# First stage reordered with x read two groups ahead; gate and memory work spread beside the forgetting heads up to the last 60 units

## The chip, the cores and the metric

The kernel runs on all 8 cores of one Trainium2 chip. Each core computes one of the 8 batch entries, with its own copy of the weights, and the cores exchange nothing. The metric is the device time in microseconds (us) of the slowest core. On a core five engines work in their own order: TensorE (PE in the profile, its weight loads PEld), VectorE (DVE), ScalarE (ACT), GpSimd (POOL), and SyncE (SP), which here only issues DMAs. An engine's queue is served in program order: an instruction that waits holds everything behind it on its engine, DMA issues included.

## What is computed

A decoder layer over 4096 tokens of width 1024: three parallel token mixers, a gated merge, an output projection and a squared-ReLU MLP.

```python
h = rmsnorm(x, g_mix[l])
proj = h @ w_in[l]                                            # (B, T, IN_WIDTH)
qa, ka, va, qb, kb, vb, fl, qm = jnp.split(proj, offs, axis=-1)
# mixer A: three groups of dilated sliding windows, merged by softmax denominators -> ya
# mixer B: forgetting attention, 8 heads, causal over all 4096 tokens
logf = jax.nn.log_sigmoid(fl.astype(jnp.float32) + b_f[l].astype(jnp.float32))
yb = fox_attention(qb, kb, vb, logf).astype(dt)
# memory cross-attention: 4 heads over 256 memory tokens -> ym
gates = jax.nn.sigmoid(h @ w_gate[l] + b_gate[l]).reshape(B, T, N_BRANCH, D)
merged = (gates[:, :, 0] * (ya @ w_br_a[l])
          + gates[:, :, 1] * (yb @ w_br_b[l])
          + gates[:, :, 2] * (ym @ w_br_m[l]))
x = x + merged @ w_out[l]
h2 = rmsnorm(x, g_mlp[l])
x = x + jnp.square(jax.nn.relu(h2 @ w_up[l])) @ w_down[l]
```

In `fox_attention` the logits of query t and key s get the sum of the log forget gates between them; the kernel adds it through six extra rows of the query and key operands, which is why its score matmuls have 70 rows.

## The kernel before

Every instruction is recorded by helpers (`MM`, `ACT`, `TT`, `STT`, `COPY`, `P.dma`; lines 238 to 268, DMAs line 59), so the profile shows their lines. `Prog.finalize` derives the semaphore waits from reads and writes. On each engine the order is the order in which the program text emits the instructions. On-chip memory is one arena of 205 KB per partition, cut by hand with `at(kb, columns)`: a new tile waits for all users of the tiles that lay there. `wcast` is a DMA issued by POOL that reads f32 weights from memory and writes bf16.

The stages on the core whose trace is shown:

- **First stage**, `phase_a` (0 to 310 us): eight token groups (`tg`) of 512 tokens. For a group, `load_x` brings eight f32 tiles of x (2 MB), `squares` squares them on ACT and sums them on POOL (chunks 0 to 4) and DVE (5 to 7) with two scratch tiles `sqs` used in turn, and ends with a sum and two roundings `shi`, `slo` on DVE; `norm` sums over partitions with two matmuls and forms 1/rms (ACT Ln, Exp); `scale` writes the bf16 `hT` with eight DVE instructions. `vproj(i, js)` multiplies a 128-token tile of `hT` by the value weights in three column blocks of 512, 256 and 512 (8 matmuls each, five banks in turn), copies them to a staging tile `vst`, and stores that to `vsc`. `p2_tg` computes the cumulated log forget gates of a group: 8 matmuls, ACT Exp and Ln, a scan and six more small instructions on DVE, and two stores to `augsc` issued by POOL. `ones_out` issues six constant stores from POOL, once. At group 4 the rotary tables (4 MB, SP) and two column groups of weights (POOL) are loaded as well.
- **Query and key projections, dilated attention** (310 to 857 us), which the change doesn't touch. The memory tokens are loaded and prepared at its start (`mem_prep`).
- **The joint loop** (857 to 1646 us): `run(...)` takes steps from several generators so that all advance in proportion: seven forgetting heads (`fox_heads(0, 7)`, 7 x 144 units), the gates (`gates`, 768 steps), memory attention (`mem_attn`, 140) and the casts of the MLP weights (`wprep`, 16). A unit of a head is a score matmul, an exponential on ACT and a value matmul. A head goes through 8 query groups of 512 tokens; group tg has 4 tg + 4 units, the last four of them narrower (512, 384, 256, 128 columns) and masked on POOL. At the end of a query group DVE takes a reciprocal and a product. Scores run three units ahead of the value matmuls.
- **The last head and the first group's merge** (1646 to 1792 us): `wcast` of the three branch weights and of `w_out`; 16 units of head 7 alone; loads of gates (`load_g`) and of the branch inputs (`load_y`); 28 more units alone; then the last 100 units beside `head_d`, that is `br_stage(0)` (eight output chunks of 2, 4 and 4 matmuls, each product with a gate on DVE, two sums on POOL) and `out_stage(0)` (eight chunks of 8 matmuls, residual sum, squares, norm, scale).
- **Rest** (1792 us to the end): the MLP with the merges of the following groups.

## Time and profile before

| | us |
|---|---|
| timed runs, in order | 3376.24, 3373.81, 2918.67 |
| their median | 3373.81 |
| the profiled execution | 2917.94 |
| its span, slowest core (the one shown below) | 2916.4 |
| spans of the 8 cores | 2897.2 to 2916.4 |
| mean granted TensorE clock, by core | 0.972 to 0.976 |

| stage | from, to (us) | PE busy |
|---|---|---|
| groups 0 to 6 of the first stage | 38.88 to 284.82 | 166.88 of 245.94 |
| projections, dilated attention | 310.04 to 856.84 | 498.99 of 546.80 |
| joint loop | 856.84 to 1645.88 | 777.85 of 789.04 |
| last head and first merge | 1645.88 to 1791.69 | 105.74 of 145.81 |
| rest, after the first 27 us | 1818.65 to 2916.40 | 1090.06 of 1097.75 |

Times count from the first instruction. The granted clock is 1.00 where TensorE runs at the upper of its two levels, 2.4 GHz, and 0.50 at 1.2 GHz. The value in brackets behind an instruction is the time its engine was idle before it, with what ended that. Matmuls overlap in the trace, so a busy share near 1 can still hide a lower clock.

### The profile page before, as it was taken

The page shows a single profiled execution, that of the slowest core. Times are in us where ns is not written, and L with a number is a line of the kernel's source. Part 1 is how long each engine was busy: PE and PEld are TensorE (multiplying, and loading weights), DVE is VectorE, ACT ScalarE, POOL GpSimd, SP SyncE. Part 2 cuts the span into 40 slices and gives each one's busy share as a digit, 9 for nine tenths or more (in the row PEclk, how much of TensorE's full clock was granted, in tenths as well). Part 3 has the DMA queues.
Part 4 walks back from the last instruction along what each step waited for, and adds up shares of the span by engine and source line. Part 5 has one row for each costly group of instructions (what it writes and reads, how often), then busy time and mean ns, then how long its engine had stood idle before and what let it go on. Part 6 is the DMA issues. An engine that isn't in the chain of part 4 may idle for free.

```text
span 2916.4 us, 45239 instructions; the slowest of 8 cores (2897.2 to 2916.4 us)
## 1 busy us (share of the span) xinstructions
PE 2687.6 (92%) x12800; PEld 1204.4 (41%) x12800; DVE 1329.3 (46%) x1761; ACT 1435.3 (49%) x2649; POOL 672.2 (23%) x770
## 2 busy tenths in 40 slices
PE   3667999998979999999999877999999999999999
PEld 1323444343434444444444322444444444444444
DVE  3444566677764655555646533323333333323221
ACT  2333455799988888887888743212121212111120
POOL 2211343343331111111101132222222222222200
PEclk9878999999999999999999989999999999999999
DMA  5363433563564454354333553464646464646353
GB/s 120 126 178 120 108 73 74 151 163 113 141 117 100 92 103 99 76 106 93 82 74 80 104 156 131 138 208 142 214 145 206 154 211 140 216 148 210 111 177 101
DMA packets 204929, 386.56 MB, mean 133 GB/s; under 512 B 82688, under 2 KB 143104, under 8 KB 181760
## 3 DMA queue, kind: packets, MB, share of 16 engines
q1 hardware_dynamic: 150640, 320.95, 34.8%
q0 software_dynamic: 51600, 56.39, 11.9%
q10 hardware_dynamic: 2448, 6.33, 0.8%
q8 instruction: 112, 1.84, 0.3%
q14 instruction: 129, 1.06, 0.1%
HBM read 328.31 MB, written 110.89 MB: 151 GB/s over the span
## 4 chain that ended last, share of the span: by engine, by line
PE 85%; DMA 4%; ACT 3%; DVE 3%; issue 2%; POOL 2%; SPq 1%; ACTq 0%; DVEq 0%; POOLq 0%
PE bank L238 85%; ACT arena L244 3%; POOL arena L247 2%; DMA arena<-xT 1%; DMA arena<-wsc_up 1%; DVE arena L257 1%; SPq L59 1%; DVE arena L261 1%; DMA arena<-ysc 1%; DVE arena L247 1%; DMA arena<-w_in 1%; DMA out<-arena 0%; DMA arena<-mem 0%; ACTq L59 0%; DMA qksc<-arena 0%
## 5 line engine op out<-in xcount | busy, mean ns | idle before, releaser
L238 PE MATMUL bank<-arena 128*128 128x512 bf16 (+6 forms) x12444 | 2629.5, 370 | 119.8 <-DVE arena L257 43.4
L238 PEld LDWEIGHTS bank<-arena 128*128 128x128 bf16 (+3 forms) x12444 | 1173.6, 98 | 1538.9 <-issue 299.7
L244 ACT ACTIVATE arena<-bank 128x512 bf16<-128x512 f32 (+2 forms) x1926 | 1012.2, 570 | 878.9 <-PE bank L238 865.8
L247 DVE TENSOR_TENSOR arena<-bank,arena 128x512 f32<-128x512 f32 (+2 forms) x528 | 373.1, 712 | 536.0 <-PE bank L238 498.7
L247 POOL TENSOR_TENSOR arena<-arena 128x512 f32<-128x512 f32 (+1 forms) x264 | 358.4, 1358 | 971.6 <-DVE arena L247 483.8
L247 DVE TENSOR_TENSOR arena<-arena 128x512 bf16<-128x512 bf16 (+5 forms) x392 | 213.7, 545 | 501.6 <-ACT arena L244 470.9
L247 POOL TENSOR_TENSOR arena<-arena,cb_sb 128x128 bf16<-128x128 bf16 (+2 forms) x352 | 212.9, 616 | 869.0 <-ACT arena L244 864.1
L244 ACT ACTIVATE arena<-arena 128x512 f32<-128x512 f32 (+2 forms) x352 | 217.2, 626 | 331.0 <-DVE arena L247 270.4
L261 DVE RECIPROCAL arena<-bank 64x512 f32<-64x512 f32 (+1 forms) x96 | 322.1, 3355 | 63.7 <-PE bank L238 61.7
L244 ACT ACTIVATE arena<-bank,gcols 128x512 f32<-128x512 f32 (+1 forms) x364 | 249.6, 686 | 202.7 <-PE bank L238 187.7
L238 PE MATMUL bank<-arena,cb_sb 128*128 128x512 bf16 (+1 forms) x340 | 110.8, 391 | 103.8 <-DVE arena L264 88.0
L253 DVE TENSOR_SCALAR arena<-arena 128x512 bf16<-128x512 f32 x192 | 82.1, 430 | 270.1 <-ACT arena L244 268.9
L257 DVE SCALAR_TENSOR_TENSOR arena<-bank,gcols,arena 128x512 bf16<-128x512 f32 (+1 forms) x196 | 152.7, 800 | 100.7 <-ACT arena L244 56.2
L257 DVE SCALAR_TENSOR_TENSOR arena<-arena,gcols 128x512 bf16<-128x512 f32 x128 | 91.0, 748 | 28.3 <-ACT arena L244 23.1
L238 PEld LDWEIGHTS bank<-arena,cb_sb 128*128 128x128 bf16 x340 | 33.3, 98 | 166.9 <-issue 135.8
L59 POOL DMA_DIRECT2D out<-arena x64 | 35.3, 552 | 289.2 <-DVE arena L247 287.1
L247 DVE TENSOR_TENSOR arena<-arena,cb_sb 128x512 bf16<-128x512 bf16 (+1 forms) x96 | 49.0, 510 | 10.0 <-ACT arena L244 6.2
L264 DVE CAST arena<-bank 128x256 bf16<-128x256 f32 x32 | 13.4, 420 | 46.8 <-PE bank L238 46.6
L59 POOL DMA_DIRECT2D augsc<-arena x22 | 12.4, 569 | 81.7 <-DVE arena L264 58.0
L264 DVE COPY arena<-bank 128x512 f32<-128x512 f32 x32 | 30.4, 1027 | 0.0
L59 POOL DMA_DIRECT2D arena<-w_gate x24 | 21.7, 909 | 24.6 <-PE bank L238 24.6
L264 DVE CAST arena<-arena 8x512 bf16<-8x512 f32 (+1 forms) x40 | 16.8, 420 | 10.9 <-POOL arena L247 7.1
(24 smaller groups left out, 61.4 us busy)
## 6 DMA issues: line engine op xcount, KB each, us to landing
arena<-wsc_up SPq DMA_DIRECT2D x64, 1024.0 KB, 5.8
arena<-wsc_dn SPq DMA_DIRECT2D x64, 1024.0 KB, 6.0
arena<-xT SPq DMA_DIRECT2D x128, 256.0 KB, 7.5
gsc<-arena SPq DMA_DIRECT2D x192, 128.0 KB, 2.0
arena<-gsc SPq DMA_DIRECT2D x64, 384.0 KB, 6.5
arena<-qksc SPq DMA_DIRECT2D x16, 1024.0 KB, 8.6
out<-arena POOLq DMA_DIRECT2D x64, 256.0 KB, 5.0
vsc<-arena SPq DMA_DIRECT2D x32, 480.0 KB, 2.7
```

The source lines that it names most:

```text
L59: self.op(eng, lambda e: e.dma_start(out=out, in_=in_, **kw), reads, writes, dma=True, nobar=nobar)
L238: P.op("pe", lambda e: e.matmul(out, lhsT=lhsT, rhs=rhs, start=start, stop=stop), reads, writes)
L244: P.op("act", lambda e: e.activation(out=out, in_=in_, func=func, **kw), reads, writes)
L247: P.op(eng, lambda e: e.tensor_tensor(out=out, in0=in0, in1=in1, op=op), reads, writes)
L253: P.op(eng, lambda e: e.tensor_scalar(out=out, in0=in0, scalar1=s1, scalar2=s2, op0=op0, op1=op1), reads, writes)
L257: P.op("dve", lambda e: e.scalar_tensor_tensor(out=out, in0=in0, scalar=scalar, in1=in1, op0=op0, op1=op1), reads, writes)
L261: P.op("dve", lambda e: e.reciprocal(out=out, in_=in_), reads, writes)
L264: P.op(eng, lambda e: e.tensor_copy(out=out, in_=in_), reads, writes)
```

## The change

In the first stage, x is read one group earlier (`load_x(tg + 2)` at the top of group tg, into the same two buffers). The squares of the next group come ahead of each of the first two `vproj`, `norm` comes after the first block of the third tile, `scale` in one piece after the third tile, and `p2_tg` at the end of the group. All three copies of a tile go to ACT, and there are three staging tiles. The constant row is shorter and read four times by a broadcast DMA.

In the joint loop all 8 heads take part, up to all but the last 60 units; the casts of two of the three branch weights are inside the loop (`wbr_early`). Behind it, `load_y(0)`, the cast of the first branch weight and three `load_g` come at once, then 16 units alone, `load_x(0)` and the cast of `w_out`, and the last 44 units beside `head_d`. The gate tiles and two product tiles move to the place of `hT`.

```diff
@@ phase_a
-        onesr, r_onesr = at1(181, T)
-        vst, r_vst = zip(*[at(189 + 4 * i, 1920, n=4) for i in range(2)])
+        onesr, r_onesr = at1(183, 1024)
+        vst, r_vst = zip(*[at(185 + 4 * i, 1920, n=4) for i in range(3)])
@@ ones_out
-                P.dma(augsc[:, 0, 3 + j, :], onesr[0:8, :], reads=[r_onesr], writes=[ra_[-1]], eng="pool")
+                o4 = onesr[0:8, :].unsqueeze(1).to_broadcast([8, 4, 1024])
+                P.dma(augsc[:, 0, 3 + j, :].rearrange("h (a t) -> h a t", a=4), o4, reads=[r_onesr], writes=[ra_[-1]],
+                      eng="pool")
@@ vproj
-                if j == 1:
-                    COPY("dve", dst, src, [rb[bk]], [r_vst[i % 2][j]])
-                else:
-                    ACT(dst, src, AF.Copy, [rb[bk]], [r_vst[i % 2][j]])
-            P.dma(vsc[i * 128:(i + 1) * 128], v, reads=list(r_vst[i % 2]), writes=[r_vsc[i]])
+                ACT(dst, src, AF.Copy, [rb[bk]], [r_vst[i % 3][j]])
+            if 2 in js:
+                P.dma(vsc[i * 128:(i + 1) * 128], v, reads=list(r_vst[i % 3]), writes=[r_vsc[i]])
@@ group loop
-            if tg:
-                load_x(tg + 1)
+            load_x(tg + 2)
             if tg == 2:
                 ones_out()
             if tg == 4:
                 load_group(0)
                 load_group(1)
                 load_tabs()
+            squares(tg + 1, 0)
             vproj(4 * tg, (0, 1, 2))
-            squares(tg + 1, 0)
+            squares(tg + 1, 1)
             vproj(4 * tg + 1, (0, 1, 2))
-            squares(tg + 1, 1)
+            vproj(4 * tg + 2, (0,))
+            norm(tg + 1)
+            vproj(4 * tg + 2, (1, 2))
+            scale(tg + 1, 0, 8)
+            vproj(4 * tg + 3, (0, 1, 2))
             p2_tg(tg)
-            norm(tg + 1)
-            vproj(4 * tg + 2, (0, 1, 2))
-            scale(tg + 1, 0, 4)
-            vproj(4 * tg + 3, (0, 1, 2))
-            scale(tg + 1, 4, 8)
@@ joint loop and what follows
-    fx = fox_heads(0, 7)
-    run((rest(fx), 7 * 144), (gt, 768), (mem_attn(), 140), (wprep(), 16))
+    wbr = [None, at(120, 4 * 1024), at(128, 4 * 1024)]
+    def wbr_early():
+        yield 1
+        for b, w_d in ((1, w_brb_d), (2, w_brm_d)):
+            wcast(wbr[b][0].rearrange("p (k c) -> p k c", k=4), w_d.rearrange("(k p) c -> p k c", p=128), [wbr[b][1][0]])
+            yield 1
+    ALONE, LAST = 16, 44
+    fx = fox_heads(0, 8)
+    nf = 8 * 144 - ALONE - LAST
+    run((take(fx, nf), nf), (gt, 768), (mem_attn(), 140), (wprep(), 16), (wbr_early(), 5))
-    Gt = [at1(120 + 3 * i, 1536) for i in range(4)]
+    Gt = [at1(4 + 3 * i, 1536) for i in range(4)]
-    wcast(wbr[:, 0:2], w_bra_d.rearrange("(k p) c -> p k c", p=128), [r_wbr[0]])
-    wcast(wbr[:, 2:6], w_brb_d.rearrange("(k p) c -> p k c", p=128), [r_wbr[1]])
-    wcast(wbr[:, 6:10], w_brm_d.rearrange("(k p) c -> p k c", p=128), [r_wbr[2]])
-    wcast(wo, w_out_d.rearrange("(k p) c -> p k c", p=128), [r_wo])
-    last = fox_heads(7, 8)
-    for _ in range(16):
-        next(last)
+    load_y(0)
+    wcast(wbr[0], w_bra_d.rearrange("(k p) c -> p k c", p=128), [r_wbr[0]])
     for n in range(3):
         load_g(n)
-    load_y(0)
-    for _ in range(28):
-        next(last)
+    for _ in take(fx, ALONE):
+        pass
     load_x(0)
+    wcast(wo, w_out_d.rearrange("(k p) c -> p k c", p=128), [r_wo])
-    tt_ = [at1(132 + 2 * i, 512, F32) for i in range(3)]
+    tt_ = [at1(kb, 512, F32) for kb in (16, 18, 136)]
-    run((rest(last), 100), (head_d(), 44))
+    run((rest(fx), LAST), (head_d(), 44))
```

## Rows read from the trace of the kernel before

**Rows 1.** The page, busy us of each engine over the whole span.

```profile
PE 2687.6 (92%) x12800; PEld 1204.4 (41%) x12800; DVE 1329.3 (46%) x1761; ACT 1435.3 (49%) x2649; POOL 672.2 (23%) x770
```

**Rows 2.** First stage by token group: window, length, busy of each engine, clock, DMA share, GB/s.

```profile
38.88:76.59 37.71, 26.33 (x106) 11.55 (x107) 16.19 (x24) 11.49 (x20) 6.26 (x6) 0.86 0.41 119
76.59:108.14 31.55, 23.11 (x107) 10.95 (x108) 16.16 (x24) 11.46 (x20) 9.26 (x12) 0.84 0.42 134
...
176.34:220.41 44.07, 23.47 (x107) 10.85 (x107) 15.52 (x24) 11.69 (x20) 6.25 (x6) 0.77 0.74 215
...
253.41:284.82 31.41, 22.22 (x106) 10.54 (x107) 16.22 (x24) 11.61 (x20) 6.19 (x6) 0.89 0.38 129
284.82:310.04 25.22, 25.22 (x124) 12.53 (x125) 6.03 (x11) 7.28 (x12) 2.05 (x3) 0.93 0.28 100
```

**Rows 3.** First stage, timeline of PE: start, length, instruction, count, idle before it.

```profile
94.89 0.59 PE L238 MATMUL bank<-arena,cb_sb 128*128 128x512 bf16 x1 [5.98 <-DVE arena L264]
...
96.06 9.83 PE L238 MATMUL bank<-arena 128*128 128x512 bf16 x48
...
239.88 11.28 PE L238 MATMUL bank<-arena 128*128 128x512 bf16 x48
```

**Rows 4.** The chain of work in time order, group 1: first and last link shown.

```profile
87.73 0.63 ACT arena L244
...
93.52 0.70 DVE arena L247
```

**Rows 5.** First stage, timeline: the norm's two ACT instructions, and eight scale instructions.

```profile
96.36 0.69 ACT L244 ACTIVATE arena<-bank,gcols 128x512 f32<-128x512 f32 x1 [4.05 <-PE bank L238]
...
97.14 0.63 ACT L244 ACTIVATE arena<-arena 128x512 f32<-128x512 f32 x1
```
```profile
31.98 6.75 DVE L257 SCALAR_TENSOR_TENSOR arena<-arena,gcols 128x512 bf16<-128x512 f32 x8 [2.35 <-ACT arena L244]
```

**Rows 6.** First stage, timeline: scan of the forget gates, and POOL's stores behind it.

```profile
63.11 1.21 DVE L450 TENSOR_TENSOR_SCAN arena<-arena 8x512 f32<-8x512 f32 x1
...
68.77 1.22 POOL L59 DMA_DIRECT2D augsc<-arena  x2 [7.77 <-DVE arena L251]
...
101.23 4.22 POOL L59 DMA_DIRECT2D augsc<-arena  x8 [7.88 <-DVE arena L264]
```

**Rows 7.** First stage: SP's issue of the first two groups of x; their landing.

```profile
1.50 43.62 SPq L59 DMA_DIRECT2D arena<-xT  x16
```
```profile
arena<-xT SPq DMA_DIRECT2D x128, 256.0 KB, 7.5
```

**Rows 8.** Joint loop and last head: windows, columns as in rows 2.

```profile
856.84:1645.88 789.04, 777.85 (x3713) 355.24 (x3713) 424.26 (x363) 654.80 (x1252) 116.54 (x253) 1.00 0.43 91
1645.88:1683.64 37.76, 22.66 (x92) 7.89 (x92) 20.73 (x11) 22.36 (x49) 9.59 (x20) 0.80 0.98 171
1683.64:1742.00 58.36, 49.56 (x195) 19.47 (x196) 24.41 (x28) 28.34 (x54) 23.37 (x24) 0.87 0.55 168
1742.00:1791.69 49.69, 33.52 (x147) 13.05 (x146) 15.74 (x16) 27.02 (x53) 11.95 (x15) 0.96 0.03 8
```

**Rows 9.** PE lines by form, 2000 to 2900 us: count, busy us, mean ns.

```profile
L238 PE MATMUL bank<-arena 128*128 128x512 bf16 x4160 | 899.0, 379 | 0.0
```

**Rows 10.** Behind the joint loop, timeline of PE: units of head 7 alone.

```profile
1649.67 10.96 PE L238 MATMUL bank<-arena 128*128 128x512 bf16 x40 [2.62 <-POOL arena L247]
```

**Rows 11.** DMA issues from 1663.7 to 1669 us: count, size, us to landing.

```profile
arena<-ysc SPq DMA_DIRECT2D x2, 512.0 KB, 24.6
```

**Rows 12.** First merge, timeline of POOL: first sum of two successive chunks.

```profile
1722.03 1.27 POOL L247 TENSOR_TENSOR arena<-arena 128x512 f32<-128x512 f32 x1
...
1726.30 1.26 POOL L247 TENSOR_TENSOR arena<-arena 128x512 f32<-128x512 f32 x1 [0.77 <-DVE arena L247]
```

**Rows 13.** End of the first output stage: its last residual sum; MLP's first matmuls.

```profile
1779.37 0.69 DVE L247 TENSOR_TENSOR arena<-bank,arena 128x512 f32<-128x512 f32 x1 [4.39 <-PE bank L238]
```
```profile
1791.69 22.14 PE L238 MATMUL bank<-arena 128*128 128x512 bf16 x84 [4.78 <-DVE arena L257]
```

More of the change, by code:

```diff
@@ L433, in ones_out @@
                 ra_.append(R())
-                P.dma(augsc[:, 0, 3 + j, :], onesr[0:8, :], reads=[r_onesr], writes=[ra_[-1]], eng="pool")
+                o4 = onesr[0:8, :].unsqueeze(1).to_broadcast([8, 4, 1024])
+                P.dma(augsc[:, 0, 3 + j, :].rearrange("h (a t) -> h a t", a=4), o4, reads=[r_onesr], writes=[ra_[-1]],
+                      eng="pool")
                 ra_.append(R())
-                P.dma(augsc[:, 1, j, :], onesr[0:8, :], reads=[r_onesr], writes=[ra_[-1]], eng="pool")
+                P.dma(augsc[:, 1, j, :].rearrange("h (a t) -> h a t", a=4), o4, reads=[r_onesr], writes=[ra_[-1]],
+                      eng="pool")
         def p2_tg(tg):
@@ L505, in vproj @@
         def vproj(i, js):
-            v = vst[i % 2]
+            v = vst[i % 3]
             for j in js:
@@ L527, in phase_a @@
         MEMSET("pool", onesr[0:8, :], 1.0, [r_onesr])
-        for i in range(2):
+        for i in range(3):
             MEMSET("pool", vst[i][:, :, 64:128], 1.0, [r_vst[i][3]])
@@ L1131, in rest @@
             yield c
-    fx = fox_heads(0, 7)
-    run((rest(fx), 7 * 144), (gt, 768), (mem_attn(), 140), (wprep(), 16))
-    wbr, r_wbr = at(0, 10 * 1024, n=3)
-    wbr = wbr.rearrange("p (k c) -> p k c", k=10)
+    wbr = [None, at(120, 4 * 1024), at(128, 4 * 1024)]
[8 more added lines that the diff above has]
+    run((take(fx, nf), nf), (gt, 768), (mem_attn(), 140), (wprep(), 16), (wbr_early(), 5))
+    wbr[0] = at(0, 2 * 1024)
+    r_wbr = [w[1][0] for w in wbr]
+    wbr = [w[0].rearrange("p (k c) -> p k c", c=1024) for w in wbr]
+    Gt = [at1(4 + 3 * i, 1536) for i in range(4)]
     wo, r_wo = at1(20, 8 * 1024)
@@ L1208, in br_stage @@
                 for kc in range(k0, k1):
-                    MM(banks[bk][:, :], wbr[:, kc, c * 128:(c + 1) * 128], yti[:, kc, :], kc == k0, kc == k1 - 1,
+                    MM(banks[bk][:, :], wbr[br][:, kc - k0, c * 128:(c + 1) * 128], yti[:, kc, :], kc == k0, kc == k1 - 1,
                        [r_wbr[br], r_yti[br]], [rb[bk]])
```

## The prediction

> **What bounds the kernel now.** I read the page first: PE is busy 92% of the span, the next engine 49% [rows 1]. So the kernel is bound by matmuls wherever its order lets it be, and the question is where PE waits. The windows by stage answer that. The joint loop keeps PE busy 777.9 of 789.0 us at a granted clock of 1.00 [rows 8]; nothing is to be had there. Two stretches are loose. In the first stage a group takes 31.4 to 44.1 us, with PE busy 22 to 26 at a clock of 0.77 to 0.89 [rows 2]. Behind the loop, 1645.88 to 1791.69 us, PE is busy 105.7 of 145.8 at 0.80 to 0.96 [rows 8]. The change works on just these two.
>
> The unit of cost is a full matmul of 512 columns: 899.0 us for 4160, 0.216 us each at the upper clock level, 2.4 GHz [rows 9]; narrower ones I count by their columns.
>
> A first-stage group holds 4 tiles of 20 full matmuls, 8 for the forget gates and 2 for the norm, 90 x 0.216 = 19.4 us. The shortest normal group takes 31.4 [rows 2]. The rest is a gap of 6 us before the norm's matmuls [rows 3] (seven of these, 6 to 18 us, the long ones behind a late x), one of 2.2 us before each new group, for the second half of `scale`, and the lower clock behind the gaps: the 48 matmuls that follow a norm are 40 full ones, 8.6 us, and take 9.8 to 11.3 [rows 3] (mean of the seven 10.4), 1.8 us too long.
>
> **First stage after the change.** Let 0 be the end of the gate matmuls of the group before; they now come last in their group. I follow the chain that leads to the next norm, queue by queue.
>
> - ACT: Exp and Ln of the forget gates, like the norm's pair 1.4 us with their hop [rows 5]; the scan starts at 1.55.
> - POOL: the stores of `p2_tg` now stand ahead of the squares' sums of the next group in POOL's queue, where before they came behind both halves. From the scan's start to the end of the two issues it is 68.77 + 1.22 - 63.11 = 6.9 us [rows 6]. POOL is held until 8.45, though ACT's first squares are done at 4.
> - The first sum ends at 9.8. The square of chunk 2 needs its scratch tile, so ACT resumes then; the copies of tile 1 wait behind it, which the five banks cover.
> - From that square to the norm's first matmul the old chain takes 94.89 - 87.73 = 7.2 us [rows 3, 4]. Nothing in it changes: first norm matmul at 17.0, both done 1.4 later at 18.4.
> - PE has had 48 x 0.216 = 10.4 us of work by then (two tiles and a block), so it still waits some 6 us here. The gap has not gone.
> - Behind it 40 full matmuls, 8.6 us, and the 1.8 us of the clock: 28.8.
> - DVE: Ln starts 1.5 us after the first norm matmul, Exp ends at 2.9 [rows 3, 5], then 0.1 + 6.75 + 0.15 for eight scale instructions [rows 5]: 26.8. That is hidden under the matmuls: the 2.2 us gap is gone, and 26.8 is the lower bound of the period.
>
> So a period of 28.8 us (26.8 to 31.5, the old normal one) for 31.4. The greater gain is that x no longer comes late: it has a whole group to land, and lands in 7.5 us [rows 7].
>
> Group 0: the second x is issued until 45.1 [rows 7] and its needed chunks land near 50 (an estimate). ACT now squares it ahead of all copies: 2.2, three copies 1.6, so chunk 2 at 53.8; with 7.2, 1.4 and 8.6 + 1.8, group 1 starts at 72.8 (for 76.59; 69 if x doesn't hold ACT). Six periods, 172.8. In group 2 six constant stores, 4.22/8 x 6 = 3.2 us [rows 6], and in group 4 two casts, taken as 1.8, stand in POOL's queue ahead of the sums too; both lay hidden before. The four times shorter pieces of the broadcast store I cost at nothing; POOL's issue is what counts. In group 4 the tables (4 MB) still stand ahead of the stores of the value tiles; in 44.1 us the old group moved 9.5 MB [rows 2], so the first store lands near 27, and the third staging tile lets ACT go on until about 24: 3 us (0 to 8). Group 7 starts at 72.8 + 172.8 + 8.0 = 253.6 for 284.8: **31.2 us gained**.
>
> Copies moved to ACT: its busy time grows from 11.5 by 4 x 0.4 us, half of the period; nothing. Forget gates last: in group 7 they delay the next stage, since the memory tokens are loaded over their tiles; at most the 5.7 us of that chain [rows 6], I take **4 lost**. The DVE part of it is over before the first projection needs DVE.
>
> **Behind the loop.** A head has 132 full units (144 units counted by columns). The 84 units that move into the loop are 75 of these, 150 matmuls: 32.4 us; the loop is 98.6% busy, so it grows by 33. ACT adds 84 x 0.55 = 46 to 654.8 of 789.0 us: 85% of 822, still no bound. The two early casts cost POOL an issue each.
>
> The remainder, from the end of the gates to the first MLP matmul:
>
> - 16 units alone, 20 take 10.96 [rows 10]: 8.8. The wait of 2.6 us before them (masks behind four casts on POOL) goes, since these units have no mask.
> - Wait for the branch inputs: landing took 24.6 us [rows 11] with three gate loads ahead and the casts beside it, 2.4 MB in all. Now they go first, 1.25 MB: 12.8 us. Issued at 3, landed at 16, gates of the first chunk at 17: a wait of 8 (0 to 15).
> - `br_stage`: a chunk with its three units is 16 matmuls, 3.5 us. But the product tile of a chunk is freed by two POOL sums one after the other: sum 1.27, 0.2, sum 1.27, then two DVE products of 0.7 and hops, 4.3 us; two successive chunks are 1726.30 - 1722.03 = 4.3 apart [rows 12], the least seen. Eight at 4.5, with one reciprocal and four masks of 4 in all: 40 (36 to 53; 53 is the mean pace of before, 6.6 a chunk).
> - `out_stage`: 8 x 12 matmuls, 20.7, say 22; two units a chunk instead of 4.5, so the wait for the exponentials, 1 us a chunk, should go (if not, 30).
> - End: 1791.69 - 1779.37 = 12.3 us [rows 13], of which 6.9 were units; now some 4.2: 9.7.
>
> Sum 33 + 8.8 + 8 + 40 + 22 + 9.7 = 121.5 for 145.8: **24.3 us gained** (3 to 40). Then up to 1818 the MLP waits for its third weight tile, loaded behind the same queue: no change.
>
> On the shared transfer the Trainium skill ("DMA: Bandwidth & Descriptors", Queues, rings and completion order) says that each DMA engine goes round between the queues that have work, packet by packet. By that rule the branch inputs get half of what moves, and at the 171 GB/s of that window [rows 8] 1.25 MB take 14.6 us (an estimate) for the 12.8 of the row: the sum would be 1.8 us longer.
>
> **Total.** 31.2 - 4 + 24.3 = 51.5; 2917.9 - 51.5 = **2866 us**. The profiled execution, 2917.9, stands 456 us below the median shown, 3373.8, and 0.7 below the shortest of the three runs; the forecast is for executions like it.
>
> **Rivals.**
>
> 1. POOL doesn't hold the squares (its sums come earlier than I count). Then the chain's start moves from 9.8 to about 5.5, the period is 24.5, and group 4 and 2 lose nothing: 6 x 4.3 + 5 = 31 more, **2835**. For: PE needs only 19.4. Against: the order in POOL's queue is plain.
> 2. The tail gives back nothing: branch inputs and `w_out` come later, and a chunk keeps its 6.6 us with fewer units beside it. 15 + 53 + 30 instead of 8 + 40 + 22: 28 less, **2894**. For: PE and DMA waits of before at the same place, DMA share 0.98 [rows 8].
> 3. The first stage keeps its normal 31.5 us a group and gains only the late x: 6 x 2.7 = 16 less, **2882**.
> 4. Slower: the denser loop and MLP, 822 + 1098 us, no longer get the upper clock throughout. It turns the sign when 1920 x (1/c - 1) passes 51.5, at a mean clock of 0.974; at the 0.93 that the densest first-stage window shows [rows 2] it costs 145, **3011**. Against: 789 us at 98.6% busy ran at 1.00 [rows 8].
>
> **How the numbers follow.** My forecast 0.51, rivals 0.14, 0.16, 0.14 and 0.05. The range leaves out rival 4 and the outer edges: 2833 to 2896. A measurement can tell 2% from no change, 58 us, so "faster" begins at 2860: rival 1 with 0.13 and the lower part of my own case (2848 to 2884), 0.24, give 0.37. Rivals 2 and 3 and the rest, 0.58. Slower, 0.05.
>
> **What will show it.** In the trace after: starts of groups some 29 us apart; before the norm's matmuls a gap of about 6 us still, and POOL's first sum right behind its two stores, 8 us into the group; no gap at the group's start; PE's clock there still below 0.9. Group 7 near 254 us. The loop ends 33 us later relative to its start; first MLP matmul 122 - 33 = 89 us after the gates' end; chunk sums on POOL 4.3 to 5 us apart. I am wrong if POOL sums before its stores, if the gap before the norm is under 3 us, or if the branch inputs land after 20 us.

## The result

The changed kernel takes 2911.19 us (median of 20 runs, 2896.75 to 3258.92), the kernel before 2931.51 beside it; ratio 0.9939 with a 95% interval of 0.9917 to 0.9962. A gain of 18 us for a forecast of 52: the same within 2%, and outside my range of 2833 to 2896. Some executions are longer, at a lower granted clock on the cores of one die or both (the 3258.92 is one); the ratios leave them out, and of e13, whose profile is one, only the cores of the other die are read. The profiled execution took 2914.3 us, its slowest core 2912.8; on the others the span is 2878.1 to 2906.6.

The page of the kernel after, busy time by engine, for [rows 1]:

```profile
PE 2686.5 (92%) x12548; PEld 1211.2 (42%) x12800; DVE 1313.5 (45%) x1729; ACT 1443.7 (50%) x2681; POOL 672.3 (23%) x771
```

This row can't tell the two kernels apart, so the stages must. I cut each trace at four marks that all kernels here have: the first norm matmul of the projections, the first matmul of head 0 behind PE's 5.2 us wait for ACT, the issue of the `w_br_a` cast on POOL (it waits for the last gate matmul), and the first MLP matmul. Each number is the mean over the eight cores of the profiled execution, in us.

| kernel | first stage | projections, windows | loop | behind it | MLP | span |
|---|---|---|---|---|---|---|
| before | 307.3 | 534.4 | 802.4 | 145.3 | 1116.8 | 2906.1 |
| after | 280.8 | 544.6 | 850.5 | 101.1 | 1121.1 | 2898.1 |
| after, profiled again (e8) | 277.8 | 539.0 | 851.5 | 100.8 | 1120.7 | 2889.8 |
| e8 less before | -29.5 | +4.6 | +49.1 | -44.5 | +3.9 | -16.3 |
| forecast | -31.2 | +4 | +33 | -57.3 | 0 | -51.5 |

(The forecast's two loop terms: the loop grows by 33, the stage behind it shrinks from 145.8 to 88.5.) The 35 us between forecast and e8 are mainly two terms: 16 in the loop, 13 behind it; the MLP has 4. Each row is one execution, and that of before is a short one: its mean span is 2906.1, where the executions of before in the ratios of the runs below have 2911.1 to 2915.8. So differences to the row of before come out 5 to 10 us too small in sum; in which stage isn't known.

The first profile of after has 544.6 us in its second column, 6 more than e8 of the same kernel. The windows of 300 to 560 us, on core 2 and on core 5 (columns as in [rows 2]):

```profile
300.00:560.00 260.00, 247.08 (x1104) 106.74 (x1125) 162.41 (x226) 144.51 (x259) 100.06 (x65) 0.92 0.43 97
300.00:560.00 260.00, 244.85 (x1195) 105.55 (x1193) 167.08 (x236) 155.48 (x280) 103.87 (x71) 0.98 0.42 96
```

Core 2 shows 0.92 of the clock and fewer instructions in the same time, core 5 shows 0.98. In e8, the same kernel, all cores show 0.98 or 0.99, so the change doesn't bring it about every time; e17 and e18 below have it on some cores again. What sets it is open. Behind the first stage I read after from core 5.

**First stage.** Timeline of PE, after, core 2 (columns as in [rows 3]):

```profile
61.88 0.38 PE L238 MATMUL bank<-arena,cb_sb 128*128 128x512 bf16 x1 [4.13 <-DVE arena L264]
...
90.58 0.59 PE L238 MATMUL bank<-arena,cb_sb 128*128 128x512 bf16 x1 [6.63 <-DVE arena L264]
...
91.83 21.82 PE L238 MATMUL bank<-arena 128*128 128x256 bf16 x102
123.56 0.59 PE L238 MATMUL bank<-arena,cb_sb 128*128 128x512 bf16 x1 [9.91 <-DVE arena L264]
```

and POOL and ACT ahead of the norm at 90.58:

```profile
80.73 1.22 POOL L59 DMA_DIRECT2D augsc<-arena  x2 [20.46 <-DVE arena L247]
81.95 1.30 POOL L247 TENSOR_TENSOR arena<-arena 128x512 f32<-128x512 f32 x1
```
```profile
83.34 1.15 ACT L244 ACTIVATE arena<-arena 128x512 f32<-128x512 f32 x2 [4.75 <-POOL arena L247]
```

The norms of groups 1 to 7 stand at 61.88, 90.58, 123.56, 152.19, 184.01, 213.25 and 243.16: periods of 28.7, 33.0, 28.6, 31.8, 29.2 and 29.9 us, 181.3 in all. POOL's sum starts the moment its two stores are issued, ACT waits 4.75 us for it, and PE 6.63 before the norm. Behind the norm PE runs without a break: the 2.2 us gap at a group's start is gone. Group 7 starts at 255.1 us here and at 252.2 on core 5 of e8 (forecast 254).

**Loop.** Windows from the loop's first to its last matmul, after, core 5:

```profile
815.95:1668.53 852.58, 826.75 (x3915) 375.89 (x3916) 454.01 (x379) 701.12 (x1350) 134.69 (x288) 0.99 0.42 90
```

In before PE was idle for 12.6 us in this stretch of core 5 (786.87 of 799.47 busy), now for 25.8. What PE waited for there: engine, releaser, us in total, times, longest. Before:

```profile
PE bank L238 <- ACT arena L244: 10.7, 9, 5.2
PE bank L238 <- POOL arena L247: 6.0, 12, 2.2
PE bank L238 <- DVE arena L261: 0.4, 2, 0.2
```

After:

```profile
PE bank L238 <- ACT arena L244: 11.2, 9, 5.2
PE bank L238 <- DVE arena L247: 10.0, 8, 3.7
PE bank L238 <- POOL arena L247: 7.6, 15, 2.9
PE bank L238 <- DVE arena L261: 1.8, 2, 0.9
```

What is new is DVE: 11.8 us for 0.4. The timeline of DVE and of PE at one such wait, core 5:

```profile
1265.48 3.35 DVE L261 RECIPROCAL arena<-bank 64x512 f32<-64x512 f32 x1
...
1269.73 3.36 DVE L261 RECIPROCAL arena<-bank 128x512 f32<-128x512 f32 x1
...
1273.58 3.36 DVE L261 RECIPROCAL arena<-bank 64x512 f32<-64x512 f32 x1
```
```profile
1277.94 6.34 PE L238 MATMUL bank<-arena 128*128 128x512 bf16 x21 [2.06 <-DVE arena L247]
```

The 64-row ones are the head's own, at the end of its token groups; the 128-row one belongs to the memory attention and has come between two of them. PE waits for the product behind the third.

**Behind the loop.** Timeline of PE, after, core 5; the gates end at 1668.53:

```profile
1669.43 7.52 PE L238 MATMUL bank<-arena 70*128 70x512 bf16 x30 [0.32 <-ACT arena L244]
1687.07 1.86 PE L238 MATMUL bank<-arena 128*128 128x512 bf16 x4 [10.12 <-DMA arena<-ysc]
1693.20 2.72 PE L238 MATMUL bank<-arena 128*128 128x512 bf16 x6 [4.26 <-DMA arena<-ysc]
1698.33 6.77 PE L238 MATMUL bank<-arena 128*128 128x512 bf16 x22 [2.42 <-DVE arena L247]
...
1738.47 20.42 PE L238 MATMUL bank<-arena 128*128 128x512 bf16 x95 [0.58 <-DVE arena L247]
...
1768.39 6.82 PE L238 MATMUL bank<-arena 128*128 128x512 bf16 x12 [4.67 <-DVE arena L257]
```

The units alone take 8.4 us (forecast 8.8). From their end at 1676.95 to 1698.33, where the branch stage begins to flow, are 21.4 us (forecast a wait of 8). The branch stage, counted from there, takes 40.1 (forecast 40), the output stage 20.4 (22), its end 9.5 (9.7). The issue of the branch inputs on SP and their landing, for [rows 11]:

```profile
1673.91 0.45 SPq L59 DMA_DIRECT2D ysc<-arena  x1
1674.51 1.78 SPq L59 DMA_DIRECT2D arena<-ysc  x3
```
```profile
arena<-ysc SPq DMA_DIRECT2D x2, 512.0 KB, 20.4
```

They are issued 6.0 us behind the gates' end, right behind a store in SP's queue, on all eight cores (forecast 3), and the last of the three lands 18.0 to 22.2 us later, by core (forecast 13). The two DMA queues from issue to landing, 1674.5 to 1694.9 us: packets, MB, share of the engines' time; software is POOL's queue with its casts, hardware is SP's.

```profile
q0 software_dynamic: 1051, 2.11, 70.2%
q1 hardware_dynamic: 1675, 1.93, 34.7%
```

### The profile page after: what moved, and what is told of

Its sections match the earlier page's. It is cut to its first block, busy times and chain, and to the rows that moved or that the text cites. A ratio compares the mean times of both kernels' runs of the same rounds, so it can differ in the third digit from the quotient of the medians.

```text
span 2912.8 us, 45013 instructions; the slowest of 8 cores (2878.1 to 2912.8 us)
## 1 busy us (share of the span) xinstructions
PE 2686.5 (92%) x12548; PEld 1211.2 (42%) x12800; DVE 1313.5 (45%) x1729; ACT 1443.7 (50%) x2681; POOL 672.3 (23%) x771
## 4 chain that ended last, share of the span: by engine, by line
PE 83%; DVE 4%; DMA 4%; ACT 3%; issue 3%; POOL 2%; SPq 0%; ACTq 0%; DVEq 0%; POOLq 0%
PE bank L238 83%; ACT arena L244 3%; POOL arena L247 2%; DVE arena L261 2%; DVE arena L247 1%; DMA arena<-xT 1%; DMA ysc<-arena 1%; DMA arena<-gsc 1%; DMA arena<-wsc_up 1%; DVE arena L264 0%; SPq L59 0%; DVE arena L257 0%; POOL augsc L59 0%; DVE arena L453 0%; DMA qksc<-arena 0%
## 5 line engine op out<-in xcount | busy, mean ns | idle before, releaser
L238 PEld LDWEIGHTS bank<-arena 128*128 128x128 bf16 (+2 forms) x12444 | 1179.3, 99 | 1530.0 <-issue 330.6
L244 ACT ACTIVATE arena<-bank 128x512 bf16<-128x512 f32 (+3 forms) x1958 | 1021.4, 567 | 830.3 <-PE bank L238 808.5
L244 ACT ACTIVATE arena<-arena 128x512 f32<-128x512 f32 (+3 forms) x352 | 216.3, 626 | 353.5 <-DVE arena L247 260.5
L244 ACT ACTIVATE arena<-bank,gcols 128x512 f32<-128x512 f32 (+2 forms) x364 | 249.8, 686 | 212.2 <-PE bank L238 193.7
L453 DVE TENSOR_TENSOR_SCAN arena<-arena 8x512 f32<-8x512 f32 x8 | 10.1, 1264 | 45.6 <-ACT arena L244 45.6
```

Of the source, the lines that this page charges most:

```text
L238: P.op("pe", lambda e: e.matmul(out, lhsT=lhsT, rhs=rhs, start=start, stop=stop), reads, writes)
L244: P.op("act", lambda e: e.activation(out=out, in_=in_, func=func, **kw), reads, writes)
L453: P.op("dve", lambda e: e.tensor_tensor_scan(out=cs_, data0=sp_, data1=sp_, initial=init, op0=ALU.add, op1=ALU.max), rd, [r_csb[k]])
```

## Which half of the change gains: e1, e2, e8

The kernel before with the new first stage only (e1), and with the new loop and stage behind it only (e2). e8 is the changed kernel again.

> The kernel before with the first stage of the change alone. Theory (my steps for the first stage held, the loss is behind it): the joint loop starts 30 us earlier, as in the changed kernel (826 against 857 us on an undisturbed core), and nothing behind it moves, so the time falls by 27 to 31 us, ratio 0.990. Rival (part of the stage's gain is given back later, by what is now nearer behind it): the loop starts 30 us earlier but the end comes only about 20 us earlier, ratio 0.993.

> The kernel before with the joint loop and what follows of the change, first stage as before. Theory (the 84 units moved cost the loop more than their matmuls, and the branch inputs land late): the loop takes 842 us for 789, the stretch behind it 100 for 146, so the time is 7 us longer, ratio 1.0025, between 1.000 and 1.005. Rival (these losses come from the new first stage, which shifts the cores against each other): loop 822, stretch 89 to 100, the time 14 to 24 us shorter, ratio 0.992 to 0.995.

> The changed kernel once more, beside the others on the same chip. Theory: 20 to 26 us shorter than the kernel before, ratio 0.991 to 0.993, the same as its undisturbed cores showed (2890 against 2916 us). Rival (its 0.9939 holds a cost of its own that undisturbed cores don't show): 0.994 or more again.

e1: ratio 0.9897 (0.987 to 0.9924), 2895.5 us, first stage 277.8 for 307.3, next column 538.2 for 534.4. e2: ratio 1.0022 (0.9999 to 1.0045), loop 850.3 for 802.4, behind it 101.5 for 145.3, MLP 1121.4 for 1116.8. e8 has two executions that can be compared, 2905.67 (the profiled one) and 2899.36 us, beside 2923.68 for before: 18 and 24 us less, and no ratio of its own. So the first stage gains what was forecast (-29.5 + 3.8 for -31.2 + 4), and the rest of the change, worth 24.3 us in the forecast, gives nothing: 47.9 - 43.8 + 4.6, some 9 us lost by the stages, 0 to 13 by the ratio's interval. In e1 the loop, which it doesn't change, takes 805.1 for 802.4.

## The loop: e5, e6, e7, e14

e5 and e6 take the memory attention's 32 reciprocals out of the kernel after and of the kernel before (its output is then not normalised):

```diff
-            RECIP(rec, banks[dk][:, :], [rb[dk]], [r_rec])
+            COPY("dve", rec, banks[dk][:, :], [rb[dk]], [r_rec])
```

> The changed kernel with each of the 32 reciprocals of memory attention (128 x 512, 3.36 us on DVE) replaced by a plain copy of about 1 us, so that its part of the output is not normalised; all else the same. Theory (two reciprocals in a row on DVE hold a bank and PE waits; the new proportions put more of them together): PE's waits in the joint loop fall from 23.8 us to under 10, and the loop from 842 to 825 to 830 us. Rival (the 20 us that the loop takes beyond its matmuls come from its DMAs or from the clock by itself): the loop stays at 838 or more.

> The kernel before with the same replacement: memory attention is not normalised. Theory (few reciprocals meet in the old proportions): the joint loop falls by 2 to 5 us only, from 789 to 784 to 787, and PE's waits from 12.1 to some 8. Rival (reciprocals cost both loops the same): it falls by as much as the changed kernel's.

(The expectations of e1, e2, e5, e6 and e7 count the loop from a later mark, 856.84 us in before: 10 us less than the columns here.) After: loop 841.4 for 851.5 in e8, 10 us less; the theory had 12 to 17, the rival at most 4. Before: 803.2 for 802.4, nothing, where I expected 2 to 5. The same 32 instructions cost 10 us in one loop and none in the other, so it isn't their number but where they fall.

e7 ends the loop behind seven heads again, with the early casts and all else as in after: 16 units of head 7, the loads, 28 units, and the last 100 beside the merge.

```diff
-    ALONE, LAST = 16, 44
+    ALONE, LAST = 44, 100
...
+    for _ in take(fx, 16):
+        pass
     load_y(0)
...
-    for _ in take(fx, ALONE):
+    for _ in take(fx, ALONE - 16):
```

> The changed kernel with the joint loop ended after seven heads as before (1008 units beside the gates), then 16 units, the loads of group 0, 28 more units alone and the last 100 beside the merge; the early casts and all else as in the changed kernel. Theory (moving the 84 units into the loop brought nothing: it grew by 53 us and the stretch behind it shrank by 46): loop 789 to 799, stretch 135 to 140, so equal to the changed kernel within 6 us, rather shorter. Rival (the move itself is worth its 24 us, and something else in the new order lost it): 15 to 25 us longer than the changed kernel.

Ratio 0.9901 (0.9878 to 0.9924). The loop reads 813.4 us, but here the mark at its end is late: the cast that sets it stands behind 16 units on POOL, which take 8.8 (by the pace of [rows 10]). Loop and stage behind it together are 944.6 us for 947.7 before and 952.3 in e8. So in the same change with seven heads in the loop the loss isn't there, and neither is the gain of 24 that moving the units was to bring.

What differs is the ratio of the streams. A head has 144 units. With 1008 units of heads over the memory stream's weight of 140, one of its 32 items (four steps each) comes every 28.8 units: exactly five a head, always at the same places. With 1092 units it comes every 31.2, 4.6 a head, and wanders through the head until it falls between the head's own reciprocals, as above. e14 changes this one number in the changed kernel:

```diff
-    run((take(fx, nf), nf), (gt, 768), (mem_attn(), 140), (wprep(), 16), (wbr_early(), 5))
+    run((take(fx, nf), nf), (gt, 768), (mem_attn(), 140 * nf / 1008), (wprep(), 16), (wbr_early(), 5))
```

> The changed kernel; one number in the joint loop: the memory attention's stream has the weight 140 x 1092/1008 = 151.7 for 140, so that one of its 32 items falls on every 28.8 units of the heads, as before the change (5 items a head of 144 units), and not on every 31.2. The theory: with 5 items a head the memory reciprocals always fall on the same places of a head, clear of the head's own; with 4.6 they drift through the head and stack on DVE, 3.36 us each. Then the loop is 8 to 10 us shorter (841 for 850 us), ratio to the kernel before 0.990. The rival: it is the share of the gates or the last head's end; the loop stays at 848 to 852 and the ratio at 0.993.

Loop 841.2 us, 10 less than e8; ratio 0.9888 (0.984 to 0.9936). Windows and waits of the loop, e14, core 5:

```profile
815.49:1658.36 842.87, 822.75 (x3915) 375.33 (x3916) 453.45 (x379) 700.68 (x1350) 133.94 (x287) 0.99 0.43 91
```
```profile
PE bank L238 <- DVE arena L247: 5.2, 4, 3.9
PE bank L238 <- DVE arena L261: 1.6, 2, 1.4
```

The same 3915 matmuls in 9.7 us less. PE's waits for DVE are 6.8 us for 11.8, and PE's busy time for the same matmuls is 4.0 less. All reciprocals run; only their places differ. That the places of the memory attention's items cost 10 us is shown, from both sides (e5 and e6, e14), and it repeats: the changed loop takes 848.6 to 853.7 us in nine profiles with the old weight (after, e2 to e4, e8 to e10, e12, e17) and 839.5 to 841.2 in three with the new one (e14, e16, e18). That the whole number is what matters is argued only: no third ratio was run, and the new weight also ends the memory attention 84 units before the loop's end. Of the loop's excess of 16 us, 10 are settled by this; some 6 stay open. A part of them is one wait of PE for DVE some 35 us into the loop: 3.7 us on core 5 of after and 3.9 in e14, but from under 1.5 to 6.4 over the cores of after, and none in the kernel before. What sets it wasn't separated.

## Behind the loop: e4, e10, e17

The branch inputs landed after 20.4 us. Beside them in that time moved the cast of `w_out` and 2 MB of x; then came 2 MB of MLP weights, all ahead of the later gates. e4 issues the cast inside the branch stage, after 3 of its 24 steps:

```diff
-    wcast(wo, w_out_d.rearrange("(k p) c -> p k c", p=128), [r_wo])
...
-        for c in br_stage(0):
+        for n, c in enumerate(br_stage(0)):
+            if n == 3:
+                wcast(wo, w_out_d.rearrange("(k p) c -> p k c", p=128), [r_wo])
             yield c
```

> The changed kernel with the cast of w_out issued behind the first chunk of the first branch stage instead of right behind the joint loop. Theory (the cast, in flight beside them, is what makes branch inputs and gates land 20 us late): they land 10 to 12 us after issue, the branch stage starts 10 us earlier, the time falls by 8 to 11 us. Rival (SP's late issue and the length of its own queue decide): they land after 17 us or more and the time falls by 0 to 3 us; and if the cast then lands too late for the output stage, it is even longer.

Ratio 0.9913 (0.9894 to 0.9932); behind the loop 97.3 us for 100.8. The landing of the inputs and PE, e4, core 5:

```profile
arena<-ysc SPq DMA_DIRECT2D x2, 512.0 KB, 10.2
```
```profile
1682.79 1.66 PE L238 MATMUL bank<-arena 128*128 128x512 bf16 x4 [3.49 <-DMA arena<-ysc]
...
1690.87 7.85 PE L238 MATMUL bank<-arena 128*128 128x512 bf16 x22 [3.74 <-DVE arena L247]
...
1713.73 2.72 PE L238 MATMUL bank<-arena 128*128 128x512 bf16 x6 [5.18 <-DVE arena L247]
...
1739.00 20.42 PE L238 MATMUL bank<-arena 128*128 128x512 bf16 x95 [0.58 <-DVE arena L247]
```

The inputs land after 10.2 us (the last of the three after 7.0 to 11.3 by core, issued 6.0 us behind the gates' end as before), PE's wait for them fell to 3.5 us and the stage flows 20.0 us behind the gates' end (1670.87 here), not 29.8, but it then takes 48.1 us: PE waits for products whose gates are late (5.18 at 1713.73). The wait had moved. The MLP is 1125.7 us for 1120.7, so that the mean span is that of e8, 2889.8, and of the 8 to 11 us expected nothing is left in the profile. e10 therefore also moves the other transfers into the branch stage, behind the gates that are needed first: the cast after 2 steps, x after 5, the two MLP tiles after 11 and 14.

```diff
-    load_x(0)
...
-    load_u(0)
-    load_u(1)
...
+            if n == 2:
+                wcast(wo, w_out_d.rearrange("(k p) c -> p k c", p=128), [r_wo])
+            if n == 5:
+                load_x(0)
+            if n == 11:
+                load_u(0)
+            if n == 14:
+                load_u(1)
```

> The changed kernel; behind the alone units only the branch inputs and the gates are loaded first, and the other transfers are issued inside the branch stage: the w_out cast after 2 of its 24 steps, the 16 tiles of x after 5, the two MLP weight tiles after 11 and 14. The theory (the tail is long since some 7 MB stand before or beside what the branch stage needs): wait for the branch inputs 8 us, as when only the cast was moved, and now no gap for gates later, so a branch stage of 40; from the gates' end to the first MLP matmul 85 to 90 us instead of 99 to 101, ratio to the kernel before about 0.990 (the changed one 0.9935, less 11 of 2920 us). The rival: the volume is the limit wherever it stands; then the wait only moves to out_stage or the first MLP tile and the tail keeps 96 to 100 us, ratio 0.992 to 0.994.

Nothing: 100.4 us for the 85 to 90 expected, ratio 0.9908 (0.9881 to 0.9936). But the edit didn't do what its text says. POOL and PE, e10, core 5:

```profile
1671.05 0.91 POOL L59 DMA_DIRECT2D arena<-w_out  x1
```
```profile
1687.74 1.86 PE L238 MATMUL bank<-arena 128*128 128x512 bf16 x4 [9.04 <-DMA arena<-ysc]
```

After 2 steps POOL has no sum of the stage in its queue yet, so the cast went out at once, 0.8 us behind that of `w_br_a`. What e10 did test is that moving x and the MLP weights alone changes nothing. e17 is e10 with `n == 3` for the cast, behind the first chunk's sums:

> e10 with the w_out cast one step later, after 3 of the branch stage's 24 steps, so that on POOL it stands behind the sums of the first chunk. Then the branch inputs have only the gates beside them, as in e4, and the later gates have no x and no MLP weights ahead of them, as in e10. The theory: wait for the branch inputs 3 to 4 us (e4) for 9 (e10), and a branch stage of 40 us, not e4's 48; from the gates' end to the first MLP matmul 88 to 93 us for the changed kernel's 101. The rival: the cast (4 MB read) moves into the same window as the later gates and holds them up wherever it stands; branch stage 46 or more, 95 to 98 us in all, as e4, and w_out itself comes late for the output stage.

POOL, the landing of the inputs and PE, e17, core 5; gates' end at 1677.62:

```profile
1698.56 0.93 POOL L59 DMA_DIRECT2D arena<-w_out  x1
```
```profile
arena<-ysc SPq DMA_DIRECT2D x2, 512.0 KB, 7.9
```
```profile
1688.66 1.03 PE L238 MATMUL bank<-arena 128*128 128x512 bf16 x4 [2.63 <-DMA arena<-ysc]
...
1694.55 8.06 PE L238 MATMUL bank<-arena 128*128 128x512 bf16 x22 [0.44 <-DVE arena L247]
...
1737.84 20.42 PE L238 MATMUL bank<-arena 128*128 128x512 bf16 x95 [0.58 <-DVE arena L247]
...
1767.76 22.43 PE L238 MATMUL bank<-arena 128*128 128x512 bf16 x81 [4.56 <-DVE arena L257]
```

Behind the loop 88.0 us (84.7 to 91.7 by core) for 100.8: the 88.5 of the forecast. From the end of the units alone (1686.03) until the stage flows are 8.5 us for my 8, and the branch stage takes 43.3 for my 40. That 8.5 meets my 8 is in part luck: the issue came 3 us later than I had it and the landing after 7.9 us for my 13. The MLP is 1119.0 for 1120.7. So both halves are needed: the cast delays the branch inputs (e17 against e10, which differ in it alone), and x and the MLP weights together delay the gates (e17 against e4). The run's ratio, 0.9909 (0.9881 to 0.9937), doesn't show the 13 us; in its profile the second column is 543.6 and the first 281.7, as in the first profile of after, with 0.91 to 0.96 of the clock between 300 and 560 us on six cores. So the gain of the stage stands by the marks alone: 88.0 us here and 89.6 in e18 below, where the ten profiles with the cast ahead of the branch stage's sums (after, e2, e3, e5, e8 to e10, e12, e14, e16) have 98.7 to 101.9.

## The first stage: e3, e9, e11 to e13, e15

The forecast named POOL's stores as what holds the norm. e3 moves POOL's DMA issues (the two stores of `p2_tg`, collected in a list `late`, the constants, the two casts) behind the squares of the next group:

```diff
+            squares(tg + 1, 1)
+            while late:
+                late.pop(0)()
             if tg == 2:
                 ones_out()
...
-            squares(tg + 1, 1)
```

> The changed kernel with every DMA issue of POOL in a group (the two stores of the forget gates, the six constant stores, the two weight casts) emitted behind the squares of the next group instead of ahead of them. Theory (POOL's queue holds the squares' sums): first norm matmul 13 instead of 19 us behind the forget-gate matmuls, period 24.8 us for 28.8, groups 2 and 4 without their extra 3.2 and 1.8, so 25 to 30 us less than the changed kernel. Rival (DVE's chain for the forget gates or the clock holds the norm anyway): the period stays above 27.5 and at most 8 us are gained.

PE, e3, core 5:

```profile
88.36 0.58 PE L238 MATMUL bank<-arena,cb_sb 128*128 128x512 bf16 x1 [4.22 <-DVE arena L264]
...
115.88 0.59 PE L238 MATMUL bank<-arena,cb_sb 128*128 128x512 bf16 x1 [4.41 <-DVE arena L264]
```

Ratio 0.9872 (0.9848 to 0.9897), first stage 264.5 for 277.8. The period is 27.5 (the theory had 24.8, the rival more than 27.5) and the gap 4.4: of 6.6 us a third is gone, and of the 25 to 30 us expected 13 came. The forget gates' chain still stands ahead of the squares' sums on DVE, and its two ACT instructions ahead of the squares. e9 moves all of it but the eight matmuls behind the squares; e11 is e9's first stage with the loop and the rest of before, e12 is e9 with e10's tail.

> The changed kernel; of the forget gates of a group only the eight matmuls stay at its end, all the rest (ACT's Exp and Ln, DVE's chain of scan and splits, POOL's stores) is emitted behind the squares of the next group, as are the six constant stores and the two casts. The theory: what holds the norm back in the changed kernel is the whole forget-gate chain ahead of the squares' sums, on POOL (2.4 us of stores and the wait for DVE) and on DVE (its chain of some 5 us ahead of its own sum). With both behind, the squares start with the group and the first norm matmul could come some 9.5 us into it, before PE has done its 10.4 us of work: the gap before the norm goes from 6.7 us to under 1.5, the period from 30.2 us (mean of six) to 22 to 24, and the run is 35 to 45 us shorter than the changed kernel (ratio to the kernel before about 0.979). The rival: moving only POOL's part brought 4.4 us of gap and periods of 27 already; if the rest is set by POOL and DVE slowing each other on their sums (1.57 us for a sum, not 0.68), the gap stays near 4 and the ratio near 0.987.

> The first stage of e9 with the loop and the stage behind it of the kernel before. If the first stage is worth what e9 expects and the loop and tail part of the change is worth nothing or a small loss, this is the fastest: 30 us (measured for the new first stage alone) and 35 to 45 more, ratio 0.975 to 0.979. By the rival of e9 it is 0.985. Against e9 itself: 0 to 8 us shorter.

> e9 and the order of transfers of e10 together: if both gains are real and lie in different stages they add, 35 to 45 and 11 us under the changed kernel, ratio about 0.975; by the two rivals 0.985 to 0.987.

e9: ratio 0.984 (0.9783 to 0.9897), first stage 258.7. e11: 0.9816 (0.976 to 0.9873), 259.0. e12: 0.9833 (0.9786 to 0.988), 258.2. PE and DVE, e9, core 5:

```profile
139.23 0.38 PE L238 MATMUL bank<-arena,cb_sb 128*128 128x512 bf16 x1 [1.77 <-DVE arena L264]
...
152.77 11.97 PE L238 MATMUL bank<-arena 128*128 128x512 bf16 x56 [3.56 <-DVE arena L257]
```
```profile
139.86 1.27 DVE L458 TENSOR_TENSOR_SCAN arena<-arena 8x512 f32<-8x512 f32 x1
...
144.97 7.54 DVE L257 SCALAR_TENSOR_TENSOR arena<-arena,gcols 128x512 bf16<-128x512 f32 x8
```

All three ratios stand above what was expected (0.979, 0.975 to 0.979, 0.975). The gap before the norm is 1.8 us, near the 1.5 expected, but the period is 27.3, not 22 to 24: the chain (139.86 to 144.97) now stands ahead of `scale` on DVE, and PE waits 3.6 us for its first tile. e13 puts the chain (ACT's and DVE's part of `p2_tg`) behind `scale`, and POOL's stores behind the squares of the group after; e15 is that first stage with the loop and the rest of before.

```diff
+            while late_s:
+                late_s.pop(0)()
...
             scale(tg + 1, 0, 8)
+            while late:
+                late.pop(0)()
             vproj(4 * tg + 3, (0, 1, 2))
```

> The changed kernel; the forget gates' elementwise chain (ACT and DVE) of a group is emitted behind the scaling of the next group's norm, and POOL's stores of it behind the squares after that. In e9, where the chain stood between the squares and the scaling, the gap before the norm fell from 6.7 to 2.3 us (1.8 and 0.5), but each group then waited 3.5 us at its start for the scaling, which DVE began only after its chain of 5.1 us; period 27.3. The theory: that 3.5 us is DVE's order; now scaling ends 5 us earlier, the wait at the group's start is gone, the period is 22 to 23.5, and the run is 22 to 30 us shorter than e9 (ratio to the kernel before 0.974 to 0.978). The rival: DVE's chain then delays its own sums of the next squares by as much, the gap before the norm comes back, the period stays at 26 to 27.5 and the ratio at 0.984.

> The first stage of e13 with the loop and what is behind it as in the kernel before. It says what the best first stage is worth by itself, without the loop: by the theory of e13 55 to 65 us (ratio 0.978 to 0.981 less the 4 us that the new loop costs, so 0.974 to 0.978); by its rival 0.9816 as e11.

PE, e13, core 5:

```profile
133.86 0.38 PE L238 MATMUL bank<-arena,cb_sb 128*128 128x512 bf16 x1 [1.77 <-DVE arena L264]
...
157.79 0.38 PE L238 MATMUL bank<-arena,cb_sb 128*128 128x512 bf16 x1 [1.78 <-DVE arena L264]
```

Periods of 23.9 us, and 104 matmuls in one run between them: the wait at the group's start is gone. The period is half a microsecond above the 22 to 23.5 expected, and group 4 with the tables still takes 31.5. First stage 245.7 (mean of cores 4 to 7), e15 244.3: 32 us under the changed kernel. The ratios, 0.9806 (0.9757 to 0.9856) and 0.9803 (0.9773 to 0.9833), missed the expected 0.974 to 0.978, because I had counted 22 to 30 us below e9 and it was 13 (245.7 for 258.7), of which the next stage gives 3 back (540.6 for 537.8). Six periods of 23.9 for 27.3 would be 20 us; but in e9 the tables' group was as short as the others, so the 7.6 us that group 4 is too long are hidden there and not here.

## Joined: e16, e18

e16 is the changed kernel with e13's first stage, e14's weight and e10's tail; e18 has e17's tail in place of e10's.

> e13, the weight of e14 and the order of transfers behind the loop of e10 (which alone gave 0 to 8 us) together. If the parts add: 22 to 30 us under e9 for the first stage, 9 for the loop, 3 for the tail, ratio 0.969 to 0.974. If one of the two theories falls, 0.978 to 0.982.

> e16 with this order of transfers behind the loop: first stage of e13, weight of e14, tail of e17. By the parts: 0 to 10 us shorter than e16 (mean span of its cores 2845.7), ratio to the kernel before 0.972 to 0.980. It is also the repeat of e16's ratio with more rounds.

| kernel | first stage | projections, windows | loop | behind it | MLP | span |
|---|---|---|---|---|---|---|
| e16 | 243.2 | 540.6 | 840.3 | 99.1 | 1122.6 | 2845.7 |
| e18 | 241.8 | 544.5 | 839.5 | 89.6 | 1118.9 | 2834.3 |

e16: 0.980 (0.9756 to 0.9844), where parts that add were to give 0.969 to 0.974; its tail was e10's, worth 2 us. e18: 2860.49 us, 0.9773 (0.9746 to 0.9799), 67 us under the 2927.42 of before beside it; its mean span is 11 us under that of e16, where 0 to 10 were expected. It beats both kernels, and the stages' gains add up: -36, -12, -11 and -2 in four stages against e8, and 5 lost in the projections. The 5 lie on two cores: 6 and 7, at 0.91 of the clock between 300 and 560 us, take 557.6 and 559.2 us there, the others, at 0.98 or 0.99, 537.7 to 543.5.

## Why the prediction was right in one half and wrong in the other

- **First stage, -31.2: right, and by its mechanism.** Periods of 28.8 with 3.2 more in group 2 and 4.8 in group 4, 180.8 us in all, against 181.3 measured (group 2 took 1 us more than forecast, group 4 2 less); gap "some 6 us", 6.6; POOL's sum right behind its two stores; no gap at the group's start; e1 alone gives -29.5. Rival 1 (24.5 us) and rival 3 (31.5) fall. Yet e3 shows that the step "POOL is held until 8.45" is only half of the reason: with POOL free the gap shrinks by 2.2 us, not by 6. The rest of the forget gates' chain, on ACT and DVE, stood ahead of the squares too; e9, which moves it as well, has a gap of 1.8. The share of each of the two engines wasn't separated.
- **The next stage, 4 lost: right in size**, +3.8 in e1. That the late forget gates are the reason wasn't tested.
- **"It grows by 33": mis-sized, +49.** I took the 84 moved units at their matmuls and checked ACT's total load. I didn't ask what the new ratio of the streams does to where DVE's reciprocals fall. The failed step is the one that let the loop grow only by the moved matmuls, because it was 98.6% busy; the places of DVE's reciprocals add 10 us to it (e14, e5). The remaining 6 are open.
- **"A wait of 8": mis-sized, 21.4 us until the stage flows.** The failed step is "Now they go first, 1.25 MB: 12.8 us": it took the inputs alone at a known rate, and left out what else moves before they land, the `w_out` cast above all. They landed after 20.4 us, which was one of my signs of being wrong ("if the branch inputs land after 20 us"); with the cast later, after 10.2 (e4) and 7.9 (e17). "Issued at 3" was wrong too: 6.0. The estimate by the Trainium skill ("DMA: Bandwidth & Descriptors", Queues, rings and completion order) was 14.6 us. The trace agrees with the half that I took from it, by bytes: SP's queue moved 1.93 of 4.04 MB until the landing, though the casts held 70% of the engines' time. But at most 1.31 MB of the 1.93 are the inputs (1.25 in units of 1024 x 1024); the gates and x issued behind them on SP moved beside them, and I had given them the whole half. Rival 2 was right in its first part (the inputs late), wrong in its other two: the branch and output stages took 40.1 and 20.4 us, as forecast, once the inputs and the first gates were there.
- **MLP, "no change": +3.9.** PE's wait for the third weight tile grew from 1.1 to 1.9 us in the mean over cores (2.5 in e2); the rest is open. e17 and e18 have 1119.0 and 1118.9, but e14, with the loads in the order of after, has 1119.5 as well, and e11, with the loop and the rest of before, has 1122.0; so neither the order of the loads nor the change is shown to be the reason.
- **Rival 4** (the clock): not seen, 0.99 over the loop of core 5.
- With the two mis-sized terms mended and nothing else (e14's weight, e17's tail), the parts sum to e8's 16.3 + 10 + 13 + 2 = 41 us, most of the 52. No run has just these two edits; e18 has them with e13's first stage.

## What to carry to other kernels

When work moves into a loop of interleaved streams, the ratio of the streams is part of the change: count the items of each stream per period of the others, and try the old ratio again when it was a whole number (here 5 items a head for 4.6 gave 10 us; no other ratio was run). When a store or a chain leaves the head of one queue, look which instruction stands behind it on each of the other queues it passes: three moves were needed here, and each showed the next wait. A DMA that is written late in the program isn't issued late unless something ahead of it in its own queue waits; read the time of the issue in the trace before judging the experiment.

## What the runs showed of the hardware

- A reciprocal of 512 columns takes DVE 3.35 us, whether on 64 or on 128 rows, five times a sum or product of 128 x 512 (0.69, [rows 13]); three of them within 11.5 us on DVE made PE wait for 2.06 us (after, core 5).
- Branch inputs of 1.25 MB landed after 20.4 us with the `w_out` cast beside them and after 10.2 (e4) and 7.9 us (e17) with that cast issued later. In the 20.4 us the casts took 70.2% of the DMA engines' time for 2.11 MB, SP's queue 34.7% for 1.93 MB.
- Between 300 and 560 us the granted clock was 0.91 or 0.92 on cores 0 to 3 of after and 0.98 to 1.00 on cores 4 to 7; the same kernel profiled again has 0.98 or 0.99 on all. By core, the projections and windows took 537.4 to 550.9 us in that execution. e18 has 0.91 on two cores only.
